# Two Blocks of a fused network: the turned mem kept in SBUF for the second Block, gate and rank columns loaded as one chunk, and a step list of its own for each Block

## What is computed

```
for l in range(2):
    u = rms_norm(x, g_pre[l]) @ w_in[l]                 # 3344 columns
    qa, ka, va, ga, qb, kb, vb, gb, rb, qm, gm = split(u)
    oa  = moba_attention(norm(qa), norm(ka), va) * silu(ga)       # 8 heads of 64
    z   = rb @ w_gate_up[l] + b_gate_up[l]              # rb: 16 rank columns
    ob  = norm(gla_attention(qb, kb, vb, log_sigmoid(z) / 16)) * silu(gb)
    mkv = rms_norm(mem, g_mem[l]) @ w_mem_kv[l]         # same mem in both Blocks
    om  = mem_attention(norm(qm), norm(mk), mv) * silu(gm)
    x   = x + concat(oa, ob, om) @ w_out[l]
```

## Time and profile before

| | |
|---|---|
| median of 3 runs | 1475.39 us (1473.96 to 1476.26) |
| the profiled execution | 1475.67 us, of which the span is 1473.7 us |
| PE busy | 1432.7 us, 97% |
| VectorE busy | 1014.4 us, 69% |
| ScalarE busy | 839.3 us, 57% |
| GpSimd busy | 97.7 us, 7% |
| HBM | 238.78 MB in DMA packets, mean 162 GB/s |
| first Block | 0 to 164 us of the span |
| second Block | 173 to 324 us |

### The profile page before, as it was taken

One profiled execution on the slowest core, in us unless ns is written; L12 is line 12 of the kernel. 1 busy time (PEld: TensorE's weight loads), 2 busy tenths in 40 slices (PEclk: granted clock), 3 DMA queues, 4 the chain that ended last, 5 costly groups with the idle time before them and its releaser, 6 DMA issues. The chain is left out here.

```text
span 1473.7 us, 20412 instructions
## 1 busy us (share of the span) xinstructions
PE 1432.7 (97%) x8107; PEld 1171.8 (80%) x8107; DVE 1014.4 (69%) x1397; ACT 839.3 (57%) x1250; POOL 97.7 (7%) x171
## 2 busy tenths in 40 slices
PE   6999899989999999999999999999999999999998
PEld 5888688878888877788887888887778778788886
DVE  6788587876556676665557666577898887766555
ACT  6646474645455554554445554458777777455443
POOL 8000000000000000000000000000230510000000
PEclk9999899999999999999999999999999999999999
DMA  7443353344565465565555556545443432565552
GB/s 234 148 139 109 119 190 124 118 131 155 187 199 173 172 213 171 161 202 194 180 192 177 199 182 191 180 159 175 150 123 94 133 104 88 157 200 177 195 182 103
DMA packets 166509, 238.78 MB, mean 162 GB/s; under 512 B 19778, under 2 KB 112608, under 8 KB 166416
## 3 DMA queue, kind: packets, MB, share of 16 engines
q1 hardware_dynamic: 164448, 233.08, 48.7%
q0 software_dynamic: 1904, 4.40, 1.1%
q10 hardware_dynamic: 64, 0.02, 0.0%
HBM read 235.89 MB, written 1.57 MB: 161 GB/s over the span
## 5 line engine op out<-in xcount | busy, mean ns | idle before, releaser
L226 DVE TENSOR_TENSOR w_lo<-raw,w_hi 128x1024 fp32r<-128x1024 f32 (+1 forms) x296 | 508.7, 1741 | 176.0 <-ACT w_hi L208 175.2
L208 ACT ACTIVATE w_hi<-raw 128x1024 fp32r<-128x1024 f32 (+1 forms) x296 | 427.2, 1461 | 193.7 <-DMA raw<-in_ffn_w_gate_up 139.7
L244 PE MATMUL A<-w_hi,x_hi 128*128 128x512 f32 (+1 forms) x640 | 261.2, 408 | 6.2 <-DVE w_lo L226 2.8
L246 PE MATMUL A<-w_hi,x_lo 128*128 128x512 f32 (+1 forms) x640 | 248.1, 388 | 0.0
L245 PE MATMUL A<-w_lo,x_hi 128*128 128x512 f32 (+1 forms) x640 | 247.4, 387 | 0.0
L244 PEld LDWEIGHTS A<-w_hi,x_hi 128*128 128x128 f32 x640 | 121.0, 189 | 38.2 <-DVE x_lo L409 6.7
L246 PEld LDWEIGHTS A<-w_hi,x_lo 128*128 128x128 f32 x640 | 120.8, 189 | 25.6
L244 PE MATMUL A<-w_hi,ffn_ffn_hT_hi 128*128 128x512 f32 x352 | 138.7, 394 | 0.0
L652 ACT ACTIVATE ffn_ffn_e<-ffn_ffn_z 128x512 f32<-128x512 f32 x44 | 27.8, 632 | 194.6 <-DVE ffn_ffn_z L686 194.6
L245 PE MATMUL A<-w_lo,ffn_ffn_hT_hi 128*128 128x512 f32 x352 | 138.4, 393 | 0.0
L245 PEld LDWEIGHTS A<-w_lo,x_hi 128*128 128x128 f32 x640 | 121.3, 189 | 20.9 <-issue 0.7
(11 more groups left out here) (385 smaller groups left out, 2119.3 us busy)
## 6 DMA issues: line engine op xcount, KB each, us to landing
raw<-in_ffn_w_gate_up SPq DMA_DIRECT2D x176, 512.0 KB, 4.6
raw<-in_ffn_w_down SPq DMA_DIRECT2D x88, 512.0 KB, 4.0
raw<-in_w_in SPq DMA_DIRECT2D x52, 512.0 KB, 4.5
raw<-in_gdn_w_in SPq DMA_DIRECT2D x48, 512.0 KB, 4.5
raw<-in_sc_w_in SPq DMA_DIRECT2D x24, 512.0 KB, 4.4
raw<-in_w_out SPq DMA_DIRECT2D x16, 512.0 KB, 4.4
raw<-in_gdn_w_out SPq DMA_DIRECT2D x16, 512.0 KB, 4.2
raw<-in_w_mem_kv SPq DMA_DIRECT2D x8, 512.0 KB, 7.8
```

The costliest lines, as they stand in the source:

```text
L208: ins = act.activation(net.w_hi[:, v % RING, part], net.raw[:, v % RING, part], ACT.Copy)
L226: ins = dve.tensor_tensor(net.w_lo[:, v % RING, part], net.raw[:, v % RING, part], net.w_hi[:, v % RING, part].bitcast(F32), ALU.subtract)
L244: pe.matmul(out, xh, hi[:, k, c, :], start=start and k == 0, stop=False)
L246: mm = pe.matmul(out, xl, hi[:, k, c, :], start=False, stop=stop and k == nk - 1)
```

## The change

Five edits, all in the Blocks.

1. **memT.** In the first Block ScalarE copies each of the four turned banks of mem to SBUF (`keep:0` to `keep:3`, four 128x512 copies), each after VectorE's `rest` of that bank. `xpre` on PE waits for all four.
2. **The second Block's mem operand** is made from memT, for all 256 tokens of one row group at a time: `next:hi:k` (ScalarE, copy with gain, 128x256) and `next:lo:k` (VectorE, 128x256), k = 0 to 7. They stand between the last `out` quarters of the first Block; the first waits until `out:1:1` has been used. `nextmem` goes: GpSimd's load of mem, 16 turns on PE, four `gain`, four `round`, four `rest`, and in the second Block ScalarE's `rms:mem` (r_mem is taken from the first).
3. **gr.** gb and rb become one chunk of 272 columns in two units of 4 row groups, after mem and before b, 48 matmuls of 272 columns. The rank columns are evacuated with r, `turn:rb` turns them, and VectorE copies the result.
4. **Waits.** A quarter of gr waits for its own group of x, not for all four.
5. **Steps.** `FIRST_ORDER` and `SECOND_ORDER` take the place of `BLOCK_ORDER`.

```diff
+    def kept_round(self, act, k, turned):
+        act.activation(self.x_hi[:, k, :], turned[:, k, :], ACT.Copy, scale=self.g[:, k:k + 1]).then_inc(self.hi.sem, 1)
+
+    def kept_rest(self, dve, k, turned):
+        dve.wait_ge(*self.hi(k + 1))
+        dve.scalar_tensor_tensor(out=self.x_lo[:, k, :], in0=turned[:, k, :], scalar=self.g[:, k:k + 1],
+                                 in1=self.x_hi[:, k, :].bitcast(F32), op0=ALU.mult, op1=ALU.subtract)\
+           .then_inc(self.lo.sem, 1)
...
-CHUNKS = {"b": (2048, 512), "gb": (2560, 256), "rb": (2816, 16), "m": (2832, 512), "qa": (0, 512), "ka": (512, 512),
+CHUNKS = {"b": (2048, 512), "gr": (2560, 272), "m": (2832, 512), "qa": (0, 512), "ka": (512, 512),
...
+FIRST_ORDER = """
+    mempre
+    unit:mem:0:0 keep:0
+    unit:mem:0:1 keep:1 lo:2:0 hi:2:0 hi:2:1
+    unit:mem:0:2 rms:mem
+    unit:mem:0:3 keep:2
+    unit:mem:1:0 keep:3 lo:2:1 hi:3:0
+    unit:mem:1:1 xpre
+    unit:mem:1:2
+    unit:mem:1:3
+    unit:gr:0:0 lo:3:0
+    unit:gr:0:1 lo:3:1 hi:3:1 evac:mem
+    unit:gr:0:2
+    unit:gr:0:3 hi:4:0 lo:4:0
+    unit:gr:1:0
+    unit:gr:1:1
+    unit:gr:1:2 lo:4:1 hi:4:1 rms:x
+    unit:gr:1:3 hi:5:0
+    unit:b:0:0 evac:gr hi:5:1
+    unit:b:0:1 norm1:mk turn:rb
+    unit:b:0:2 z lo:5:0 lo:5:1
+    unit:b:0:3 hi:6:0
...
+    unit:b:1:3 norm2:mk lo:6:0 lo:6:1 hi:6:1 decay hi:7:0 evac:b hi:7:1 kexp
+    unit:m:0:0 turn:qkb lo:7:0 hi:8:0 turn:mk lo:7:1
+    unit:m:0:1 spread
...
+    unit:m:1:0 lo:8:0 lo:8:1
+    unit:m:1:1 hi:8:1
+    unit:m:1:2
+    unit:m:1:3 levels:0:0
...
+    out:0:0:0 lo:19:0
+    out:0:0:2 hi:19:1 hi:20:0 cturn:1 lo:19:1
+    out:1:1:2
+    out:1:1:3 next:hi:0 hi:20:1 lo:20:0 lo:20:1
+    out:0:0:1 next:hi:1 next:hi:2 next:lo:0 next:lo:1 next:lo:2 next:hi:3 next:lo:3
+    out:0:0:3 add:0
+    out:1:0:0 next:hi:4 next:hi:5 lo:21:0 next:hi:6 hi:21:0 hi:21:1 lo:21:1
+    out:1:0:1 next:lo:4 next:lo:5 next:lo:6 next:hi:7 next:lo:7
+    out:1:0:2
+    out:1:0:3 add:1
+""".split()
...
+SECOND_ORDER = """
+    hi:2:0
+    unit:mem:0:0
+    unit:mem:0:1 hi:2:1
+    unit:mem:0:2 hi:3:0 lo:2:0 hi:3:1
+    unit:mem:0:3 lo:2:1
+    unit:mem:1:0 xpre
+    unit:mem:1:1 lo:3:0
+    unit:mem:1:2 rms:mem evac:mem
+    unit:mem:1:3 hi:4:0 hi:4:1 lo:3:1
+    unit:gr:0:0 rms:x
...
+    out:1:0:2 hi:21:1 lo:20:1 lo:21:0 add:1
+    out:1:0:3 lo:21:1
+""".split()
...
-            elif kind == "nextmem" and self.next is not None:
-                pe.wait_ge(*self.cat_lo(4))
-                pe.wait_ge(*self.probs(len(self.items)))
-                pe.wait_ge(*self.next.mem_loaded(16))
-                self.next.mempre.pe(pe)
             elif kind == "xpre":
-                pe.wait_ge(*(self.mempre.gained(4) if self.prev is not None else self.mempre.lo(4)))
                 if self.prev is None:
+                    pe.wait_ge(*self.mempre.lo(4))
+                    pe.wait_ge(net.mem_kept, 4)
...
+                    if c == "gr":
+                        pe.wait_ge(*self.xpre.lo(self.xpre.groups.index((q // 2, h)) + 1))
+                    w.unit(net.x_hi, net.x_lo, 4 * h, 4, CHUNKS[c][1], banks, h == 0, h == 1, quarter=q)
...
+            elif step[0:2] == ("next", "hi") and self.next is not None:
+
+                if step[2] == "0":
+                    act.wait_ge(net.unit_used, self.u_out + 2)
+                self.next.mempre.kept_round(act, int(step[2]), self.memT)
+            elif kind == "keep" and self.prev is None:
+                n = int(step[1])
+                act.wait_ge(*self.mempre.lo(n + 1))
+                bank = self.mempre.banks[n][:, :].rearrange("p (k t) -> p k t", k=4)
+                act.activation(self.mempre.part(self.memT, n), bank, ACT.Copy).then_inc(net.mem_kept, 1)
```

More of the change, by code:

```diff
@@ new lines @@
+    unit:qa:0:2 hi:10:0 hi:10:1
+    unit:qa:0:3 levels:0:1 hi:11:0 norm1:qm
+    unit:qa:1:0
+    unit:qa:1:1 lo:10:1 hi:11:1
+    unit:qa:1:2 levels:0:2
+    unit:qa:1:3 hi:12:0 lo:11:0 evac:qa
+    unit:ka:0:0 norm2:qm glav:0 gate1:b glav:1 gate1:m hi:12:1 lo:11:1 levels:1:0 norm1:qa
+    unit:ka:0:1 lo:12:0 hi:13:0
+    unit:ka:0:2
+    unit:ka:0:3 hi:13:1 levels:1:1
+    unit:ka:1:0
+    unit:ka:1:1 lo:12:1
+    unit:ka:1:2 hi:14:0 levels:1:2 turn:qm evac:ka
+    unit:ka:1:3
+    unit:va:0:0 glav:2 lo:13:0 glav:3 norm2:qa turn:qa1 gcopy hi:14:1 scores:8
@@ L763 @@
     unit:b:1:1 decay
     unit:b:1:2
[L765 to L778, removed]
+    unit:b:1:3 hi:6:0 hi:6:1 hi:7:0 lo:6:0 lo:6:1 evac:b hi:7:1
@@ L779 @@
+    unit:m:0:0 mempre kexp lo:7:0 turn:qkb norm2:mk hi:8:0 lo:7:1
+    unit:m:0:1 hi:8:1 spread lo:8:0
+    unit:m:0:2 turn:mk
+    unit:m:0:3
+    unit:m:1:0 hi:9:0 lo:8:1 hi:9:1 hi:10:0
+    unit:m:1:1
+    unit:m:1:2 levels:0:0 evac:m
+    unit:m:1:3 gate1:b norm1:qm lo:9:0 hi:10:1
+    unit:qa:0:0
     unit:qa:0:1 lo:9:1
-    unit:qa:0:2 hi:10:0 hi:10:1 hi:11:0 hi:11:1 levels:0:1 lo:10:0 lo:10:1
-    unit:qa:0:3 hi:12:0
-    unit:qa:1:0
+    unit:qa:0:2 hi:11:0
+    unit:qa:0:3 lo:10:0 levels:0:1
@@ L790 @@
     unit:ka:1:0
-    unit:ka:1:1
-    unit:ka:1:2 levels:1:2
-    unit:ka:1:3 lo:12:1 lo:13:0 hi:14:1 glav:2 glav:3 evac:ka scores:8
+    unit:ka:1:1 turn:qm
+    unit:ka:1:2 hi:13:0 levels:1:2 hi:13:1 evac:ka
+    unit:ka:1:3 lo:12:1 glav:2 hi:14:0 glav:3 scores:8 gcopy
     unit:va:0:0
[L795 to L799, removed]
@@ L813 @@
[L813 to L821, removed]
+    unit:va:0:1 norm1:gla lo:13:0 lo:13:1
+    unit:va:0:2 hi:14:1 pturn:8 norm1:ka scores:10 pturn:9
+    unit:va:0:3 hi:15:0 hi:15:1 turn:qa0 lo:14:0 lo:14:1
+    unit:va:1:0 norm2:gla
@@ L822 @@
+    out:0:1:0 pv:2
+    out:0:1:1 lo:17:1
+    out:0:1:2 pturn:4 gate2:a scores:6
+    out:0:1:3 join:2 lo:18:0 hi:19:0 pv:3
+    out:1:1:0 pturn:5
+    out:1:1:1 hi:19:1 jgate:2 lo:18:1 pv:4 pturn:6 cturn:0 pv:5 join:3 pturn:7 pv:6 pv:7 hi:20:0
+    out:0:0:0 jgate:3
+    out:0:0:2 cturn:1 hi:20:1
+    out:1:1:2 lo:19:0
+    out:1:1:3 lo:19:1
+    out:0:0:1 add:0 hi:21:0
+    out:0:0:3 lo:20:0
     out:1:0:0
-    out:1:0:1 lo:21:0 lo:21:1
-    out:1:0:2
-    out:1:0:3 add:1 nextmem
+    out:1:0:1
@@ L1344, in unit_end @@
                 n += 1
[L1345 removed]
+                if step[1:3] == (c, "1"):
                     return n
@@ L1361, in dve @@
                 dve.wait_ge(*self.mempre.lo(4))
-            elif kind == "nextmem" and self.next is not None:
-                self.next.mempre.dve(w)
+            elif step[0:2] == ("next", "lo") and self.next is not None:
+                self.next.mempre.kept_rest(dve, int(step[2]), self.memT)
             elif kind == "xpre":
```

169 lines of the change are left out of this document (90 added, 79 removed).

## The result

The changed kernel takes 1461.28 us (median of 4 runs, 1460.12 to 1464.56), the kernel before in the same series 1474.68 us (1472.19 to 1476.26). The ratio is 0.9914, with a 95% interval of 0.9892 to 0.9937. Two later series of the same changed kernel gave 1461.88 and 1460.25 us. The forecast was 1460.4.

What follows compares the result with a forecast made beforehand. PE's own matmul starts plus a few waits were taken to bound the kernel; 9.1 + 2.4 + 4.8 + 2.4 - 3.0 - 0.4 = 15.3 us off 1475.67 gave 1460.4, range 1456.5 to 1465.5.

Steps and rivals of the forecast that it cites:

- Between the Blocks, 9.1 + 2.4: Second Block's first mem unit starts at 164.3 instead of 173.4, 9.1 us; its first 12 matmuls at full clock, 2.4 us.
- The second mem unit does not wait: Second Block: unit 21 lands 4.6 us after issue, at 161.3, so no wait; 1.8 us if its landing is unchanged.
- gr, 2.4 per Block: Both Blocks: dropping rb saves 2.74 us, 48 matmuls of 272 columns cost 0.34 more; net 2.4 each, 4.8 us.
- 2.4 + 0.3 - 0.4: Second Block: gr's 2.4 us, the 0.3 us wait before rb gone, 0.4 us lost at four more breaks for small work.
- The waits before rb, 2.4: PE's waits for all four groups of x, 2.06 us in the first Block and 0.3 in the second, both go: 2.4 us.
- New waits, 3.0: Waits before `xpre`, gr's second unit, b and `levels:0:0`, from later lists and PE coming sooner: 0 to 4 us, taken as 3.0 lost.
- The rival that the lists keep up: Both Blocks' new step lists cause no new wait, only the 0.4 us loss: 18.3 us saved, 1457; chance 0.22.
- the one that they owe more: Chains to `levels` stick to VectorE, so both Blocks lose gr's gain: 8 to 10 us saved, 1466 to 1468; chance 0.15.
- 2.4 + 2.1 less the new waits: First Block: gr's net 2.4 us and the 2.06 us wait before rb gone, less the waits the new lists bring.
- Into the FFN, nothing: Feed-forward entry: `add:1` ahead of `lo:21:1` lets PE's last 8 turns begin 1.2 us sooner, but the first matmul starts unchanged.
- The clock at the FFN: Rival: turns that cut the 3.4 us gap at the feed-forward entry keep the clock up, about 0.8 us more, 1459.5; chance 0.08.

Runs made afterwards that it cites:

- nextmem_back: Changed kernel with the second Block loading and turning mem again behind `add:1`; gr and the unread first-Block copies stay: 1472.25 us, ratio 0.9991.
- behind: Changed kernel with the sixteen `next` steps moved behind `lo:21` and `add:1` in ScalarE's and VectorE's lists: 1467.23 us.
- dummy_load: Changed kernel with GpSimd's load of mem put back in its old place, its data unread: 1464.82 us.
- wait_all: Changed kernel with gr's first matmul of each Block waiting for all four groups of x instead of its own: 1464.32 us.
- after: The changed kernel's profiled execution in the first series, the slowest of its four: 1464.56 us, span 1462.5; the series' median is 1461.28 us.
- boundary_only: Kernel before, gb and rb kept, with only memT, the copies and next steps added and the first Block's `rms:x` moved: 1466.68 us, ratio 0.9947.
- filled: Changed kernel with twelve unread matmuls put into PE's two waits at the FFN's entry, four and eight: 1458.95 us.
- after_again: The changed kernel unaltered, run again as base of a later series: 1461.88 us, ratio 0.9917; profiled span 1456.5.
- after_third: The changed kernel unaltered, run once more as base of the series with the filled waits: 1460.25 us.

## Why the prediction was right, and where its terms were not

The sum came to 15.3 us, from 1475.67. The medians differ by 13.4, and the forecast of 1460.4 is 0.9 us from the result. A part of that nearness is luck: the 1475.67 that the sum starts from is 1.0 us above the median of before, which hides half of the 1.9. Several terms are off, in both directions.

- **Between the Blocks, 9.1 + 2.4.** Measured 9.1 and about 2.5. `nextmem_back` shows that this is nearly the whole gain, `behind` that 4.3 us of it are the place under the output; 4.1 of the rest are unit 21's earlier landing, since mem's operand stood behind that unit. The prediction had put the 9.1 to the place alone and kept the load for the second mem unit.
- **The second mem unit does not wait.** Right, with unit 21's load landing in 4.2 us where I took 4.6. `dummy_load` shows that the load of mem had caused the delay: 7.7 us with it, and 8.3 in the kernel before.
- **gr, 2.4 per Block.** 48 matmuls at 0.126 us, forecast 0.127. In the second Block 148.0 became 145.9; the sum had 2.4 + 0.3 - 0.4, less its part of the new waits. Right.
- **The waits before rb, 2.4.** This is the step that was wrong under the right total. "Both go" is true of the old waits, but gr's early start meets the bank that mem's eviction still holds, a wait that I had not listed, and later bounds behind it. By `wait_all`, asking for one group at a time is worth 0.4 us in the second Block; in the first it moves b by 0.4 to 0.9, of which nothing can be told by the Block's end.
- **New waits, 3.0.** Measured in the first Block: 0.3 to 1.4 before `xpre`, 0.7 for the bank, 0.2 before b, 0.5 before `levels:0:0` and some 0.25 before `turn:qkb`, together 2.0 to 3.0; in the second none that is listed. So the size was right and the list wrong: b waits 0.2 and not 0.7 to 0.9, gr's second unit not at all. The rival that the lists keep up was wrong in the first Block, the one that they owe more in both. The first Block gained 1.5 us, where its part of the sum (2.4 + 2.1 less the new waits) gives 1.5 to 2.5; up to 1 us of that is not traced.
- **Into the FFN, nothing.** It is 1.2 us shorter in after (5.5 against 6.7), 1.2 to 1.5 in all the others. It isn't the new place of `add:1`: boundary_only has the old order there and 5.4 us. ScalarE has the weights of unit 21 at 308.15, 2.1 us before PE's last output matmul starts (310.26), before 1.0 (322.87 against 323.82), and in boundary_only 2.3 (312.42 against 314.71). Why that load lands sooner was not tried.
- **The clock at the FFN.** I had given 0.08 to its staying up there, and counted nothing for its falling for longer. In after it falls for 6.8 us. The rule of the Trainium skill that I named ("TensorE: Matmul & The Clock Gate", "Part 1: The HAM clock gate": throttled by default, released by activity) agrees with what `filled` shows, but I drew the wrong thing from it: cutting the gap in two, into waits of about 1 and 2 us, did not keep the clock up in nine of the eleven profiles that had them, and filling both did in the two that were tried.

So the right total holds, beside the waits, two misses of opposite sign. One is the 1.2 us before the FFN. The other is half clock elsewhere: outside the 5.3 us between the Blocks it cost the profile of before 6.8 / 2 = 3.4 us; the three profiles of the changed kernel have 17.0 / 2 = 8.5, 3.4 / 2 = 1.7 and 10.2 / 2 = 5.1, 5.1 in the mean. Of the 2.5 us that the clock gave between the Blocks 1.7 are so given back, with a wide spread. Whether that follows from the change stays open. In before and nextmem_back, where PE stands still for 9 us between the Blocks, the second Block has no later stretch of half clock. Of the eleven profiles with a gap of 0.2 us six have one between 225 and 232 us (dummy_load has another at 208), and so has `behind`, with a gap of 4.5. That is too few to tell.

Where these stretches begin is plainer. In all profiles together eleven begin inside a Block away from the gap and from the start, and each begins within 0.6 us of the end of the same work, 32 small matmuls of `levels` that PE does in 2.0 us, in the first Block or in the second. In after:

```profile
223.81 2.00 PE L1188 MATMUL G<-block_QE,block_KE 32*128 32x64 f32 x32
225.74 0.55 PE L245 MATMUL A<-w_hi,x_hi 128*128 128x512 f32 x1
226.08 0.63 PE L246 MATMUL A<-w_lo,x_hi 128*128 128x512 f32 x1
```

Most executions of the same work are followed by full clock, and no experiment changed it, so this is where the clock fell, not a cause shown.

The stages' own gains (1.5 + 9.1 + 2.1 + 1.2 = 13.9) and the net clock (0.8) make 14.7. The three profiled spans of the changed kernel average 1459.6, 14.1 under before's 1473.7, and the medians differ by 12.4 to 13.4; what is left is within what the executions differ by.

## What to carry to other kernels

Moving a preparation pays where an engine stands still, and its place in the queues can be worth as much as doing less: the same sixteen copies were worth 5.3 us more ahead of two steps than behind them, and leaving out the load and turns of mem 5.0, mostly by letting another load land sooner. When a wait is removed, look for the next holder of the same resource (here the accumulation bank): a start 1.6 us earlier became 0.4 to 0.9 at the next chunk, and nothing that can be told at the end of the Block. A step of a shared list is moved for all engines at once: here `rms:x`, which holds ScalarE's sum of squares, took two memsets of VectorE with it into a place where PE waited for VectorE. And two parts that are sized apart need not add up.

## What the runs showed of the hardware

- Most of the run-to-run spread of this kernel goes with the granted clock. Away from the old gap, the start and the kernel's end, the stretches of half clock in the profiles lasted 3.4 or 6.8 us; one of 3.4 us costs about 1.6 us under matmuls (147.5 against 145.9). Up to PE's last matmul, after_again has 3.4 us of it at a span of 1456.5, after 17.0 us at 1462.5. Of the 15 runs of the changed kernel those at a mean clock of 0.999 took 1457.1, 1458.4 and 1460.1 us, those at 0.994 took 1464.0, 1464.4 and 1464.6.
- The clock fell where PE had not stood still: in after at 226 us, behind 32 small matmuls (32x64, 2.0 us) and with no listed wait. In after_third the same work at the same place ran at full clock.
- A 1 MB load on GpSimd's queue delayed two 512 KB pieces on SP's queue from 4.2 to 7.7 us to landing (medians of the two pieces, one profile each).
